# A transformer kernel: mean squares of the first mixer split into two products, its recurrence one tick later, a scaled residual moved to GpSimd

## The reference, cut to what matters

```python
def rmsnorm(x, g):
    y = xf * lax.rsqrt(jnp.mean(xf * xf, axis=-1, keepdims=True) + EPS)
    return (y * g).astype(x.dtype)
# first block
a = rmsnorm(h, attn_norm[i]); proj = a @ w_in[i]
oa = hgrn2_mixer(aq, af, ai, ag, ...)          # 4 recurrent heads
ob = fox_mixer(bq, bk, bv, bf, ...)            # qh = rmsnorm(heads(q)), kh = rmsnorm(heads(k))
oc = moba_mixer(cq, ck, cv, ...)               # the same norms
h = h + concat([oa, ob, oc]) @ w_out[i];  ...  # then a conv FFN and a gated embedding
# second block: another mixer, then
hn = rms_norm(h, ffn_norm)
q = (hn @ w_query); scores = einsum('thcd,hckd->thck', q, sub_keys)   # top 16 of 128, twice
act = gelu(einsum('thkd,td->thk', expert_down[idx], hn));  out = einsum('thk,thkd->td', gates * act, expert_up[idx])
```

## Time and profile before

| | us |
|---|---|
| median of 3 runs | 3022.6 (3022.4 to 3023.23) |
| the profiled execution's own time | 3024.05 |
| its span, first to last instruction | 3022.3 |

### The profile page before, as it was taken

The page is one execution under the profiler, slowest core; times in us unless marked ns, Lnnn a source line. Parts: engine busy times, 40 slices in busy tenths (PEclk is TensorE's granted clock), DMA queues, the critical chain, the costliest instruction groups (busy, mean ns, idle before and its releaser), DMA issues.

```text
span 3022.3 us, 42696 instructions
## 1 busy us (share of the span) xinstructions
PE 3001.1 (99%) x16864; PEld 2643.9 (87%) x16864; DVE 2337.0 (77%) x3532; ACT 1686.8 (56%) x2546; POOL 466.6 (15%) x316
## 2 busy tenths in 40 slices
PE   9999999999999999999999999999999999999999
PEld 7888888888888888888898889999999988888887
DVE  5577767777776454568767699999999888999987
ACT  6455655444444344555565545599965555555544
POOL 1000000000000000000000000033333333655661
PEclk9999999999999999999999999999999999999999
DMA  7543444555555555555334656788899999999996
GB/s 259 189 160 126 147 166 178 189 190 189 188 189 190 197 188 190 188 186 181 126 140 163 218 174 224 267 293 299 292 327 356 353 357 364 400 387 386 386 387 257
DMA packets 199927, 728.81 MB, mean 241 GB/s; under 512 B 22320, under 2 KB 22448, under 8 KB 199088
## 3 DMA queue, kind: packets, MB, share of 16 engines
q1 hardware_dynamic: 162144, 587.72, 53.9%
q0 software_dynamic: 37360, 136.79, 12.3%
q10 hardware_dynamic: 224, 1.57, 0.2%
HBM read 721.34 MB, written 4.19 MB: 240 GB/s over the span
## 4 chain that ended last, share of the span: by engine, by line
PE 91%; DVE 6%; ACT 2%; DMA 1%; issue 0%; SPq 0%; DVEq 0%; ACTq 0%
PE b L2210 90%; DVE wlo L1333 2%; DVE ar L1322 1%; ACT ar L656 1%; PE b L2218 1%; DMA raw<-in_w1v 1%; ACT whi L660 1%; DVE ar L1330 0%; DMA raw<-in_dn 0%; DVE ar L1936 0%; DVE ar L1931 0%; DVE ar L1327 0%; DVE ar L1944 0%; DVE ar L1928 0%; DVE ar L1939 0%
## 5 line engine op out<-in xcount | busy, mean ns | idle before, releaser
L1333 DVE TENSOR_TENSOR wlo<-raw,whi 128x1024 fp32r<-128x1024 f32 x1053 | 1275.9, 1221 | 446.2 <-ACT whi L660 442.2
L2210 PE MATMUL b<-aa,whi 128*128 128x512 f32 (+2 forms) x5024 | 1441.6, 366 | 4.3 <-DVE wlo L1333 4.2
L660 ACT ACTIVATE whi<-raw 128x1024 fp32r<-128x1024 f32 (+1 forms) x1054 | 1094.6, 1053 | 528.5 <-DMA raw<-in_up 206.0
L2210 PE MATMUL b<-aa,wlo 128*128 128x256 f32 (+1 forms) x4640 | 1037.5, 267 | 0.0
L2210 PEld LDWEIGHTS b<-aa,wlo 128*128 128x128 f32 x4640 | 876.8, 189 | 99.1 <-issue 2.4
L2210 PEld LDWEIGHTS b<-aa,whi 128*128 128x128 f32 x5024 | 837.7, 189 | 15.5 <-issue 11.2
L2210 PE MATMUL b<-whi,asb 128*128 128x512 f32 x1230 | 412.1, 389 | 0.0
L2210 PE MATMUL b<-whi,aa 128*128 128x512 f32 x1024 | 323.1, 394 | 4.8 <-DVE wlo L1333 2.2
L2210 PE MATMUL b<-wlo,asb 128*128 128x512 f32 x820 | 319.0, 389 | 0.0
L646 POOL DMA_INDIRECT aaf<-in_up,ex x128 | 259.2, 2025 | 173.9 <-DVE aaf L1330 167.9
L2210 PEld LDWEIGHTS b<-whi,asb 128*128 128x128 f32 x1230 | 230.8, 188 | 47.9
(11 more groups left out here) (198 smaller groups left out, 2867.3 us busy)
## 6 DMA issues: line engine op xcount, KB each, us to landing
raw<-in_dn SPq DMA_DIRECT2D x256, 512.0 KB, 5.4
raw<-in_up SPq DMA_DIRECT2D x205, 512.0 KB, 7.2
raw<-in_wgu SPq DMA_DIRECT2D x176, 512.0 KB, 3.6
raw<-in_wdn SPq DMA_DIRECT2D x88, 512.0 KB, 3.7
raw<-in_w1fm SPq DMA_DIRECT2D x74, 512.0 KB, 4.4
raw<-in_w2fm SPq DMA_DIRECT2D x74, 512.0 KB, 3.6
raw<-in_wo SPq DMA_DIRECT2D x64, 512.0 KB, 3.6
raw<-in_plg SPq DMA_DIRECT2D x32, 512.0 KB, 3.6
```

Of the source, the lines that this page charges most:

```text
L660: return e.activation(o, i, ACT.Copy)
L1333: return e.tensor_tensor(o, a, high.bitcast(F32), ALU.subtract)
L2210: return e.matmul(o, l, r, start=start, stop=stop)
```

## The change

1. In the 12 heads of the first mixer, ScalarE copies the square to fp32r (`LWr[n]`), GpSimd subtracts that from the square (`SQr[n]`, fp32r, in place), and TensorE multiplies a fp32r matrix of 1/128 with each of the two and adds in PSUM, instead of one float32 product. TensorE now waits for GpSimd's count in `e_v[n]`; GpSimd waits for the ScalarE copy. Counts move from 8 and 10 a head to 9 and 11.
2. `hgrn` has one more `yield` on ScalarE and VectorE and TensorE, ahead of its first product: all the recurrence that follows is a tick later on each of the three.
3. `HS` and `HS2` are made by GpSimd, in four instructions (residual times gains for both, then times the 1/rms for both), and VectorE's two are gone. GpSimd waits for the gains, for the copy of the residual and for ScalarE's use of it.

```diff
+            arr = sb("ar1r", 25856, FR, ph)
+            avg1 = sb("avg1", 128, FR, ph)
+            SQr = [arr[:, 22016 + i * 512:22528 + i * 512] for i in range(NB)]
+            LWr = [arr[:, 23552 + i * 768:24064 + i * 768] for i in range(NB)]
...
 # gpsimd
+            e.memset(avg1[:, :].bitcast(F32), 1.0 / 128)
...
+            for hd in range(12):
+                n, r = hd % NB, hd // NB
+                e.wait_ge(e_a[n], 9 * r + 2)
+                e.tensor_tensor(SQr[n], SQb[n], LWr[n].bitcast(F32), ALU.subtract).then_inc(e_v[n], 1)
+
             e.wait_ge(n_sq, 32)
...
-            e.wait_ge(s_hs, 1)
+            e.wait_ge(s_hd, 32)
+            e.wait_ge(s_sk, 48)
+            e.wait_ge(w_y, 4)
+            e.wait_ge(n_v, NV[4] + 6)
+            both = ((HS[0:TS, :], slice(0, 1024)), (HS2, slice(1024, 2048)))
+            for o, r in both:
+                e.tensor_tensor(o, h[0:TS, 0, r], GR[:, r], ALU.mult).then_inc(s_hs, 1)
+            e.wait_ge(s_hs, 2)
+            for o, r in both:
+                e.tensor_scalar(o, o, small[0:TS, 12:13], None, ALU.mult).then_inc(s_hs, 1)
+            e.wait_ge(s_hs, 4)
             e.dma_start(HS[TS:128, :], HS2).then_inc(s_hsd, 16)
...
 # scalar: hgrn (the same in vector's and tensor's hgrn)
                 yield
+                yield
                 for li in range(8):
...
 # scalar: head
                 act(SQb[n], qk, ACT.Square).then_inc(a, 1)
+                e.wait_ge(a, 9 * r + 1)
+                cp(LWr[n], SQb[n]).then_inc(a, 1)
                 yield
                 yield
-                rs_rows(SQb[n], LW[n][:, 0:512], B[5 + n], (p, 4 * r + 1), a, 8 * r + 1)
+                rs_rows(SQb[n], LW[n][:, 0:512], B[5 + n], (p, 4 * r + 1), a, 9 * r + 2)
...
 # vector, after the query tiles
-            e.wait_ge(s_hd, 32)
-            e.wait_ge(s_sk, 48)
-            e.wait_ge(w_y, 4)
-            stt(HS[0:TS, :], h[0:TS, 0, 0:1024], small[0:TS, 12:13], GR[:, 0:1024], ALU.mult, ALU.mult)
-            stt(HS2, h[0:TS, 0, 1024:2048], small[0:TS, 12:13], GR[:, 1024:2048], ALU.mult, ALU.mult).then_inc(s_hs, 1)
...
 # tensor: head
-                means(b, [SQb[n]], (a, 8 * r + 1), p)
+                e.wait_ge(v, 11 * r + 1)
+                mm(b, avg1[:, :], LWr[n], True, False)
+                mm(b, avg1[:, :], SQr[n], False, True).then_inc(p, 1)
```

More of the change, by code:

```diff
@@ L313, in build @@
         with ExitStack() as ph:
+            arr = sb("ar1r", 25856, FR, ph)
+            avg1 = sb("avg1", 128, FR, ph)
+            SQr = [arr[:, 22016 + i * 512:22528 + i * 512] for i in range(NB)]
+            LWr = [arr[:, 23552 + i * 768:24064 + i * 768] for i in range(NB)]
+        with ExitStack() as ph:
             sb("below_fs", 6144, FR, ph)
@@ L497, in out1_done @@
                 return h_v, 64 + 4 * (q // 2)
-            return e_a[(q - 4) % NB], 8 * ((q - 4) // NB + 1)
+            return e_a[(q - 4) % NB], 9 * ((q - 4) // NB + 1)
         def out2_done(q):
@@ L891, in head @@
                 yield
-                e.wait_ge(v, 10 * r + 7)
+                e.wait_ge(v, 11 * r + 8)
                 act(lg[:, 0:128], lg[:, 0:128], ACT.Exp, bias=c[:, 0:1], acc=c[:, 2:3]).then_inc(a, 1)
@@ L1578, in head @@
                 yield
-                rs_rows(SQb[n], LW[n][:, 0:512], b, (a, 8 * r + 4), v, 10 * r)
+                rs_rows(SQb[n], LW[n][:, 0:512], b, (a, 9 * r + 5), v, 11 * r + 1)
                 yield
-                e.wait_ge(v, 10 * r + 2)
+                e.wait_ge(v, 11 * r + 3)
                 for j in range(2):
@@ L1594, in head @@
                     stt(lg, DIST, SLOPES[hd - 6], b[:, 0:384], ALU.mult, ALU.add).then_inc(v, 1)
-                e.wait_ge(v, 10 * r + 5)
+                e.wait_ge(v, 11 * r + 6)
                 e.tensor_reduce(c[:, 0:1], lg[:, 0:128], AX.X, ALU.max, negate=True).then_inc(v, 1)
@@ L1599, in head @@
                 yield
-                e.wait_ge(a, 8 * r + 6)
+                e.wait_ge(a, 9 * r + 7)
                 e.reciprocal(c[:, 4:6], c[:, 2:4]).then_inc(v, 1)
-                e.wait_ge(v, 10 * r + 8)
+                e.wait_ge(v, 11 * r + 9)
                 ts(lg[:, 0:128], lg[:, 0:128], c[:, 4:5], None, ALU.mult).then_inc(v, 1)
@@ L2446, in head @@
                 if r:
-                    e.wait_ge(a, 8 * r)
+                    e.wait_ge(a, 9 * r)
                 e.wait_ge(s_k, 7)
-                means(b, [SQb[n]], (a, 8 * r + 1), p)
+                e.wait_ge(v, 11 * r + 1)
+                mm(b, avg1[:, :], LWr[n], True, False)
+                mm(b, avg1[:, :], SQr[n], False, True).then_inc(p, 1)
                 yield
@@ L2454, in head @@
                 yield
-                e.wait_ge(v, 10 * r + 4)
+                e.wait_ge(v, 11 * r + 5)
                 if fox:
@@ L2469, in head @@
                 yield
-                e.wait_ge(v, 10 * r + 10)
+                e.wait_ge(v, 11 * r + 11)
                 for i in range(3):
@@ L2477, in head @@
                 vo = 512 + hd * 128
-                e.wait_ge(a, 8 * r + 7)
+                e.wait_ge(a, 9 * r + 8)
                 av_T(b, V1[:, 0, vo:vo + 128], V1[:, 1, vo:vo + 128], wt).then_inc(p, 1)
```

## The result

| | us |
|---|---|
| kernel before, median of 9 runs | 3022.6 (3021.51 to 3023.35) |
| changed kernel, median of 9 runs | 3031.55 (3030.13 to 3034.08) |
| ratio, with its 95% interval | 1.0029 (1.0021 to 1.0038) |
| profiled execution of the changed kernel | 3034.08, span 3032.3 |

The change costs 9 us, 0.3%: more than can be mistaken for no change. The forecast was 3023.0 with a range up to 3028.0, so it was wrong: the measured time lies 3.5 us above the range. The profiled execution is the slowest of the nine, 2.5 us above the median.

What follows compares the result with a forecast made beforehand. The prediction took TensorE to bound the kernel, except VectorE from 1774 to 1840 us. Terms -4.4 - 0.8 + 5.7 + 0.1 - 0.15 = +0.45 us on the 3022.6 median gave 3023.0 us, range 3014.5 to 3028.0.

Steps and rivals of the forecast that it cites:

- the sum: Whole kernel: terms -4.4 - 0.8 + 5.7 + 0.1 - 0.15 = +0.45 us, giving 3023.0 us.
- What bounds it: TensorE bounds the recurrence and heads, at clock 1.00; VectorE bounds 1774 to 1840 us.
- (a): First mixer's mean squares: two fp32r products replace one float32, 0.40 us less each; eleven counted, -4.4 us.
- (b1): Recurrence one tick later: first product's 1.70 us wait goes, head 0's mean square waits for the subtraction; net -0.8 us.
- (b2), the heads: Mean squares of heads 2, 3, 5, 6, 8 wait 0.8, 0.4, 0.8, 0.7, 3.0 us for the added chain: +5.7 us.
- (b2), the level products: Seven later level products of the recurrence: two multiplications end 2.8 us after the tile, so 0.1 us in all.
- (b2), the end of the mixer: End of the first mixer: the forecast had no term for it, 0 us.
- (c): Scaled residual near 1800 us: VectorE spared 2.45 us but held 2.3 by GpSimd, net -0.15 us.
- the sign: Near 1795 us: a VectorE L1333 instruction taking over 2.5 us would show the forecast right.
- The one on the slower side: GpSimd's subtraction starts up to 1.2 us later behind two-input VectorE instructions, residual +1.7: +6.8 us, 3029.4, chance 0.10.
- A new idle at the level products: Recurrence's level products: TensorE idling there anew was listed as a sign that the forecast is wrong.
- the first rival: All covers hold, nothing is held: -9.0 us, 3013.6; with head 0's wait -7.3, 3015.3; chance 0.20.

Runs made afterwards that it cites:

- the run with the later rsqrt: Changed kernel with ScalarE's three rsqrt instructions of heads 0 and 3 one tick later, behind the copy of the tile's second half: 3027.7 us, ratio 1.0015.
- the run without part 2: Changed kernel with the added `yield` on ScalarE, VectorE and TensorE undone, split means and GpSimd residual kept: 3019.07 us, ratio 0.9987.
- the run of part 2 alone: Kernel before with only one more `yield` in the recurrence on ScalarE, VectorE and TensorE: 3027.76 us, ratio 1.0017.
- the runs that filled it: Changed kernel with useless TensorE products ahead of waits: at level 1 and head 8, 3031.35 us; at level 0 and head 8, 3029.73 us.

## Why the prediction was wrong, step by step

The ledger has 9.8 us that the sum had not. 3.9 are the waits of the level products, which is the step that failed; 3.2 are the slow clock behind two waits, which the sum put at nothing; 2.1 are the end of the mixer, for which it had nothing.

- **What bounds it.** Right in that TensorE bounds the first mixer. "A product costs its columns", from a clock of 1.00 in every stretch, was a statement on the kernel before, whose longest idle was 1.70 us; the change made longer ones (2.16 and 2.99), with a clock of 0.51 and 0.69 behind them. In the profiled execution that was 3.2 us; in another the same idles may cost nothing more.
- **(a)** Right: 0.40 a head, eleven times the same step in the trace. Where nothing is waited for, two products and their way to the next weights take 0.46 (209.65 to 210.11).
- **(b1)** Right: the 1.70 are gone, head 0 waits 1.49 (1.4). GpSimd's 128x512 subtraction took 1.27 to 1.33 in nine of twelve (1.25), and 1.54 to 1.66 in three.
- **(b2), the heads.** Right, in mechanism too: the trace has 0.56, 0.26, 0.56, 0.55 and 2.99 us of idle at heads 2, 3, 5, 6 and 8, for 0.8, 0.4, 0.8, 0.7 and 3.0. At head 2 the level's multiplications (219.85 to 221.75) stand ahead of the maxima, and the square starts at 223.78, 4.8 us later than in the kernel before, while the weights ahead of the mean square come 3.0 later: 1.8 us of cover lost, for 1.9. One head that I gave full cover (10) waits 0.34.
- **(b2), the level products.** This step failed: "two multiplications end at 1.5 (the fold) + 1.3 = 2.8 after it: 0 to 0.1 each". The 1.5 was read from a tile of the kernel before, in which ScalarE stood idle for the copy. I had moved VectorE's multiplications by a tick in my head and left ScalarE's Exp where it was, though the diff moves it by the same tick. Behind that Exp come the rsqrt instructions, the rounding and VectorE's low part, and with them the fold ends 3.8 us after the tile (198.24 to 202.08) and not 1.5. The two multiplications behind it end at 5.0, and TensorE is there at 2.9. The waits at levels 0 and 4 (2.16 and 1.10 us of idle, 3.8 from start to start) came of it, and 1.7 of slow clock behind the first. It is the error that the run with the later rsqrt isolates: it takes 3.9 us back.
- **(b2), the end of the mixer.** 2.1 us not forecast. The 0.86 of the output product's first addition is VectorE held by GpSimd: the wait comes and goes with the subtraction on GpSimd. In the run without part 2, VectorE's two instructions beside it are

```profile
393.84 1.66 POOL L621 TENSOR_TENSOR ar1r<-ar,ar1r 128x512 fp32r<-128x512 f32 x1 [10.05 <-ACT ar1r L683]
...
394.26 1.92 DVE L1355 SCALAR_TENSOR_TENSOR ar<-ar,small 128x256 f32<-128x256 f32 x2
```

and took 0.87 in the kernel before; TensorE idled 0.59 for it. I had asked whether VectorE holds the subtraction, in a rival, and not what the subtraction holds. In the changed kernel one two-input instruction of VectorE is 0.2 to 1.1 us longer beside each of the twelve subtractions; behind the last alone does TensorE then idle for VectorE. The 0.67 at the recurrence's output stands in the run of part 2 alone too, so it is the shift's; its link was not followed. Head 10's 0.57 wasn't either.
- **(c)** Right in size, wrong in parts: 2.5 us held (2.3), 2.45 spared, net within 0.2 of nothing, with the VectorE instruction of 3.04 us that was named as the sign. The two-input product took 2.38 where it ran free (2.3), but the scaling took 2.84 each, where I had 1.0 from a memset's step, and it held VectorE as well. The Trainium skill, "SBUF — State Buffer", section "Who interferes with whom", names any GpSimd instruction that reads SBUF beside a two-input one of VectorE; that agrees with the 3.00 in place of 2.36 here, and a GpSimd instruction holding VectorE, which no row of before showed at that length, is shown here by 3.04 in place of 1.22.
- **The rivals.** The one on the slower side had another mechanism (the subtraction starting late behind VectorE): the subtraction took up to 0.4 longer in three of twelve places, none of them a wait of TensorE's for it. "A new idle at the level products" stood among the signs that would make the prediction wrong, and it was the sign that came; it had 0.1 us in the sum and no price or chance among the rivals, and it should have been one. The 3015.3 beside the first rival adds 1.7 us for head 0's wait, where the working has 1.4: it should be 3015.0.

## What to carry to other kernels

When a `yield` moves a step, it moves that step on every engine that has it: redraw each engine's order around it, and take no interval from the old trace whose ends lie on two sides of a moved instruction. A cover is spent once: two edits that are each priced against the same slack cost more together (6.6 us here) than the sum of both. And a wait ahead of TensorE has two prices, its length and what the clock may do behind it; moving the one product that waits, on TensorE alone, gave the gain that moving everything lost.

## What the runs showed of the hardware that I had not expected

- **The clock behind an idle.** I collected every idle of TensorE of over 1 us between 180 and 440 us from all twelve traces. Behind the 29 of 1.05 to 1.71 us the granted clock of the next 3.5 us was 1.00 each time. Of the 16 from 2.08 to 4.52 us, 13 were followed by 0.50 to 0.72, and three (two of 2.17, one of 2.99) by 1.00. So an idle of the same length in the same place may cost nothing or some 1.5 to 1.7 us more. That the idle is the cause is argued from this list; the runs that filled it don't prove it. The Trainium skill, "TensorE: Matmul & The Clock Gate", part 1, says that the throttled state is the default and activity releases it, and that the moment of the change varies from run to run; the traces agree so far as the clock fell only behind the longer idles, and behind 2.16 us in one execution and not behind 2.17 in another.
- **GpSimd's arithmetic.** 128x512 two-input: 1.27 to 1.33 us where it does not wait for VectorE. 64x1024 two-input: 2.38 for the one that starts first, 3.37 for the one that starts beside VectorE's low part. 64x1024 with one SBUF input and one scalar: 2.84, more than with two inputs.
- **VectorE held.** Its own record grows (3.04 for 1.22, 2.98 for 1.89, 1.92 for 0.87): it shows up as a long instruction, not as idle time. A search for idle time alone misses it.
